# A two-layer decoder trunk in split float32: VectorE makes the low parts of all weight units, GpSimd none

## The reference

```python
for layer in range(DEPTH):                       # DEPTH = 2
    a = rmsnorm(h, attn_norm[layer])
    h = h + hybrid_mixer(a, w_in[layer], ..., w_out[layer])
    m = rmsnorm(h, ffn_norm[layer])
    if layer % 2 == 0:
        h = h + swiglu(m, dense_w_gate[i], dense_w_up[i], dense_w_down[i])
    else:
        h = h + moe_swiglu(m, router_w[i], moe_w_gate[i], moe_w_up[i], moe_w_down[i])
return rmsnorm(h, final_norm)

def swiglu(h, wg, wu, wd):
    return (jax.nn.silu(h @ wg) * (h @ wu)) @ wd
```

## Time and profile before

| | us |
|---|---|
| median of 3 runs | 2337.15 (2335.81 to 2337.19) |
| profiled execution, device time | 2332.12 |
| its span, first to last instruction | 2330.5 |
| mean granted clock of TensorE | 0.985 of full speed |

### The profile page before, as it was taken

One profiled execution on the slowest core, in us unless ns is written; L12 is line 12 of the kernel. 1 busy time (PEld: TensorE's weight loads), 2 busy tenths in 40 slices (PEclk: granted clock), 3 DMA queues, 4 the chain that ended last, 5 costly groups with the idle time before them and its releaser, 6 DMA issues.

```text
span 2330.5 us, 29151 instructions
## 1 busy us (share of the span) xinstructions
PE 2244.1 (96%) x10281; PEld 1830.2 (79%) x10281; DVE 1563.3 (67%) x1712; ACT 1239.3 (53%) x1529; POOL 383.4 (16%) x209
## 2 busy tenths in 40 slices
PE   7999999999999999999999999999979999999994
PEld 5888788888888888888877888877758777777773
DVE  4466675666655566666554457666769999989996
ACT  4445454454444344444444445444547777777774
POOL 2121212222222222222212121121200000000002
PEclk9999999999999999999999999999979999999997
DMA  6454535555555655555554445444669999999996
GB/s 225 159 169 156 181 127 182 170 174 198 183 195 180 201 192 185 196 195 183 181 180 162 163 146 179 154 172 163 215 236 378 375 373 387 379 378 374 373 383 220
DMA packets 261545, 525.46 MB, mean 225 GB/s; under 512 B 15044, under 2 KB 15144, under 8 KB 259944
## 3 DMA queue, kind: packets, MB, share of 16 engines
q1 hardware_dynamic: 248832, 497.33, 61.3%
q0 software_dynamic: 6256, 27.00, 3.1%
q10 hardware_dynamic: 6392, 0.25, 0.2%
HBM read 511.96 MB, written 15.73 MB: 226 GB/s over the span
## 4 chain that ended last, share of the span: by engine, by line
PE 77%; DVE 7%; DMA 7%; issue 4%; ACT 4%; POOL 1%; ACTq 0%; DVEq 0%; SPq 0%; POOLq 0%
PE acc L1399 20%; PE acc L1401 20%; PE acc L1400 20%; PE acc L1677 3%; PE acc L1679 3%; PE acc L1678 3%; DVE w_lo L893 3%; DMA raw<-in_moe_w_gate 2%; ACT w_hi L603 2%; DMA raw<-in_moe_w_up 2%; DMA raw<-in_moe_w_down 1%; PE X L1507 1%; PE X L1416 1%; PE X L1427 0%; PE X L1525 0%
## 5 line engine op out<-in xcount | busy, mean ns | idle before, releaser
L893 DVE TENSOR_TENSOR w_lo<-raw,w_hi 128x1024 fp32r<-128x1024 f32 x801 | 995.6, 1263 | 534.4 <-ACT w_hi L603 532.7
L603 ACT ACTIVATE w_hi<-raw 128x1024 fp32r<-128x1024 f32 x939 | 977.3, 1057 | 663.7 <-PE acc L1401 554.6
L1399 PE MATMUL acc<-w_hi,a_hi 128*128 128x512 f32 x1600 | 631.6, 395 | 8.6 <-POOL w_lo L510 4.7
L1401 PE MATMUL acc<-w_hi,a_lo 128*128 128x512 f32 x1600 | 625.3, 391 | 0.0
L1400 PE MATMUL acc<-w_lo,a_hi 128*128 128x512 f32 x1600 | 624.5, 390 | 0.0
L510 POOL TENSOR_TENSOR w_lo<-raw,w_hi 128x1024 fp32r<-128x1024 f32 x138 | 336.0, 2435 | 1333.8 <-ACT w_hi L603 1023.3
L1399 PEld LDWEIGHTS acc<-w_hi,a_hi 128*128 128x128 f32 x1600 | 301.7, 189 | 73.0 <-issue 6.8
L1401 PEld LDWEIGHTS acc<-w_hi,a_lo 128*128 128x128 f32 x1600 | 301.1, 188 | 63.9
L1400 PEld LDWEIGHTS acc<-w_lo,a_hi 128*128 128x128 f32 x1600 | 301.6, 188 | 60.3
L1677 PE MATMUL acc<-w_hi,a_hi 128*128 128x512 f32 x768 | 310.7, 405 | 8.9 <-DVE w_lo L893 7.9
L1679 PE MATMUL acc<-w_hi,a_lo 128*128 128x512 f32 x768 | 301.1, 392 | 0.0
(11 more groups left out here) (225 smaller groups left out, 1404.7 us busy)
## 6 DMA issues: line engine op xcount, KB each, us to landing
raw<-in_w_in SPq DMA_DIRECT2D x112, 1024.0 KB, 4.9
raw<-in_moe_w_gate SPq DMA_DIRECT2D x64, 1024.0 KB, 7.1
raw<-in_moe_w_up SPq DMA_DIRECT2D x64, 1024.0 KB, 5.7
raw<-in_moe_w_down SPq DMA_DIRECT2D x64, 1024.0 KB, 5.6
raw<-in_dense_w_gate SPq DMA_DIRECT2D x44, 1024.0 KB, 5.0
raw<-in_dense_w_up SPq DMA_DIRECT2D x44, 1024.0 KB, 5.0
raw<-in_dense_w_down SPq DMA_DIRECT2D x44, 1024.0 KB, 5.1
raw<-in_w_out SPq DMA_DIRECT2D x32, 1024.0 KB, 5.1
```

The source lines that it names most:

```text
L603: nc.scalar.activation(w_hi[:, slot], raw[:, tile % RAW_SLOTS, u % TILE_UNITS], ACT.Copy)\
L893: nc.vector.tensor_tensor(w_lo[:, slot], raw[:, (u // TILE_UNITS) % RAW_SLOTS, u % TILE_UNITS], w_hi[:, slot].bitcast(F32), ALU.subtract). ...
L1399: nc.tensor.matmul(dst, hi, w_hi[:, slot, c], start=first and c == 0, stop=False)
L1401: ins = nc.tensor.matmul(dst, lo, w_hi[:, slot, c], start=False, stop=last and c == UNIT_CHUNKS - 1)
```

## The change

GpSimd's loop of low parts goes, with its semaphore, and VectorE's `split_lo` no longer skips those units. One semaphore counts all low parts, so a waiter for unit `u` waits for `u + 1`.

```diff
-POOL_UNIT = 3
...
-        def pools(u):
-
-            return u < M0 and u % 4 == POOL_UNIT
-
         def low_ready(eng, u, per=0, i=None):
 
-            if u >= M0:
-                eng.wait_ge(lo_ready, lin(3 * M0 // 4 + u - M0 + 1, per, i))
-            elif pools(u):
-                eng.wait_ge(pool_ready, lin(u // 4 + 1, per // 4, i))
-            else:
-                eng.wait_ge(lo_ready, lin(3 * (u // 4) + u % 4 + 1, 3 * per // 4, i))
+            eng.wait_ge(lo_ready, lin(u + 1, per, i))
...
-            def low_parts(u, per, i):
-
-                pool.wait_ge(hi_ready, lin(u + 1, per, i))
-
-                low_ready(pool, u - 1, per, i)
-                nc.gpsimd.tensor_tensor(w_lo[:, u % SPLIT_SLOTS],
-                                        raw[:, (u // TILE_UNITS) % RAW_SLOTS, u % TILE_UNITS],
-                                        w_hi[:, u % SPLIT_SLOTS].bitcast(F32), ALU.subtract).then_inc(pool_ready, 1)
-
-            with pool.Fori(0, M0 // 8) as i:
-                low_parts(POOL_UNIT, 8, i)
-                low_parts(4 + POOL_UNIT, 8, i)
...
             def split_lo(u, per=0, i=None):
 
-                if pools(u):
-                    return
                 slot = u % SPLIT_SLOTS
```

More of the change, by code:

```diff
@@ L254, in trunk @@
         lo_ready = sem("lo_ready")
-        pool_ready = sem("pool_ready")
         used = sem("used")
```

## The result

The changed kernel takes 2351.6 us (median of 5 runs, 2344.3 to 2354.2) against 2335.8 for the kernel before beside it (5 runs); the ratio is 1.0063, with a 95% interval of 1.0045 to 1.0081. In a second set of runs it was 2350.4 against 2336.6, 1.0051 (1.0035 to 1.0067). So the change costs 12 to 15 us. The forecast was 2349, in a range of 2340.5 to 2357: direction, size and range held. Its terms held less well: the sum of them was 2 to 4 us short, and behind that stand misses of both signs; that is what the rest is about.

The account below looks back on a forecast made before the run. TensorE, busy 2244.1 of 2330.5 us, was taken to lose time only where it waits. The terms summed to +11.9 on the profiled 2332.1, giving 2344.0; with the 5.0 offset to the median, 2349, range 2340.5 to 2357.

Parts of the forecast that it names:

- Steady gate: Dense loop, ten trips: VectorE's longer queue makes its second add late, TensorE waits 0.56, 0.65 with restart: +6.5 us.
- First gate: Before the dense loop, once: one unit's length lost, +2.7 us, and a clock drop behind the 3.4 us gap, +1.7.
- Start: First weight tiles: GpSimd's spare-row copies, issued at 6 us, share the transfer engines; +5 us, bounds -1.4 to +9.
- rival 1: The start costs its upper end: +16 us in all, 2353; chance 0.17.
- Attention: Both layers, second and third quads: VectorE's chain and units gain 1.0 and 0.75 us per layer, together -3.5.
- Router: End of the second attention layer: VectorE's product no longer beside GpSimd's low part, router starts 0.5 us earlier: -0.5.
- Expert layer: Has no GpSimd low parts and was forecast to stay as it is.
- rival 2: The steady gate in the dense loop doesn't stall: +5.4 us in all, 2342.5; chance 0.15.
- rival 4: Only the gates pay: start near its lower end, no clock drop: +3.8 us in all, 2341; chance 0.12.
- rival 3: Not slower: VectorE freed of GpSimd's turns, start untouched, gate doesn't stall: -2.7 us, 2334.5; chance 0.08.

Follow-up runs that it names:

- Experiment 5: The changed kernel with GpSimd's copies held back and the dense loop gate's second reciprocal and product two units later: 2332.6 us, ratio 0.9973 to the kernel before.
- experiment 6: The control: the kernel before, GpSimd's low parts kept, with only the loop gate's second reciprocal and product two units later: 2337.0 us, ratio 1.0004.
- experiment 1: The changed kernel with GpSimd's three spare-row copies moved behind its wait for the end of both attentions: 2339.6 us, ratio 1.0008 to the kernel before.
- experiment 4: Against the kernel before, GpSimd keeps its low parts in both attention layers only (72 of 138), VectorE makes the dense layer's: 2348.4 us, ratio 1.0047.
- experiment 3: Against the kernel before, GpSimd keeps its low parts in the dense layer only (66 of 138), VectorE makes the attention's: 2326.2 us, ratio 0.9944.
- experiment 2: The kernel before with the three spare-row copies put ahead of GpSimd's loop of low parts, nothing else changed: 2346.8 us, ratio 1.0037.
- experiment 8: The changed kernel with copies held back, second reciprocal later and one low part inside the first gate: 2327.7 us, ratio 0.9950 to the kernel before.
- experiment 9: The kernel of experiment 8 run a second time: 2327.8 us, ratio 0.9959 to the kernel before.
- experiment 7: The changed kernel with copies held back and one low part between the first gate's two reciprocals: 2337.5 us, ratio 1.0003 to the kernel before.

## Why the prediction was right, and where it wasn't

*Steady gate: +6.5 forecast, +8.4 measured, mechanism shown.* The chain was right to 0.01 us, the wait 0.55 for 0.56. What was mis-sized is what a wait costs beyond itself: I took 0.09 for TensorE's restart, and it is 0.29 (each trip is 0.84 longer: 8.4 in ten). About half of that is how the trace counts: products here start 0.23 apart, so the one behind 582.12 was due at 582.35 and started 0.71 late, at 583.06, while the idle time in the row counts only from the end of the product before. The rest is that the next ones follow at 0.33 and 0.24 us. Experiment 5 removes it whole, the control shows that it is the order.

*First gate: +2.7 and +1.7 forecast, +5.6 measured.* The wait itself cost 2.7 (3.39 us between where the unit could have started and where it did, less the 0.67 of before). The granted clock fell as forecast, but the half clock lasted twice the 3.4 us forecast, in both executions of the kernel after; in experiments 1, 4 and 5, with the same wait, it lasted 3.4 (4.1 to 4.4 us lost in all). That this drop goes with the long wait is shown at this place: in five executions a wait of 3.2 us had it, in the eight others 1.45 us or less had none. A long wait isn't enough everywhere: in experiment 3 TensorE waited 3.46 us at the start (until 30.66), and the next 9 us were at full clock.

*Start: +5.0 forecast, +8.0 and +8.9 measured at unit 4.* This is the term that was mis-sized most: the upper end of its bounds, so rival 1 was right on the mechanism. I took 5 since "the first tile is nearly in by then". The first high part was indeed only 2.0 us late (13.90 for 11.88), but the second tile had all of the copies against it, and ScalarE's DMA issues stand behind its high part. The fourth high part came 8.50 us late (36.85 for 28.35), just the 8.5 us of extra traffic; but 7.0 of it came with the tile and only 1.5 with the issues, where the upper bound had all of it. Copies and weights did share by packets: 743 and 630 from 10 to 22 us, in packets of 3.9 and 2.0 KB (2.90 MB / 743, 1.25 MB / 630), so that the weights had 30% of the bytes. By the Trainium skill (DMA: Bandwidth & Descriptors, Queues, rings and completion order) engines go round the queues a packet at a time; the trace agrees with that (from 14 to 22 us the packets are 496 and 481), and the upper end that this would give is what came. Experiments 1 and 2 show the cause from both sides.

*Attention: -3.5 forecast; the sites forecast gave -4.8.* Per layer the unit at the second quad starts 1.62 us earlier after the one before it (3.08 us for 4.70) and that at the third 0.77 (3.08 for 3.85), in both layers alike. The second was forecast as 0.75. The first was forecast as 1.0, what the chain gains; but the transposes before the unit went from waiting 0.69 to not waiting, and behind them the unit's own wait and its restart went too. Experiment 3 keeps this gain, 4 gives it up.

*Router: -0.5 forecast, +0.5 of gain measured at the wait, 1.4 in all.* The product beside GpSimd's last low part took 3.19 us and 1.22 after. TensorE's wait ahead of the router's first transposes is 2.07 us in all four executions where GpSimd makes the low parts of the second attention (the kernel before, experiments 2, 4 and 6) and 1.57 in the nine others: the 0.5 of the forecast. What it left out is the clock. Right behind the longer wait the granted clock is at half its level for 3.4 us in each of those four (in the kernel before 0.50 from 1688.0 to 1691.4), and in none of the nine; without it and the 0.5, the transposes of the router's logits start 12.35 us behind unit 551 where it was 13.70, 1.4 earlier. Further on, each execution has one more long stretch at half the clock, of 17 to 24 us, whose length changes from one to the next; that is why experiment 4 gains 1.8 at units 552 to 554 without having the shorter wait.

*Expert layer: 0 forecast, +5.3 in the profiles.* Here the prediction had an unseen help. Of thirteen profiled executions the one of the kernel before had the shortest expert layer. All others are longer, by 1.8 to 8.1 us, among them experiments 2 and 6 (1.8 and 3.0), whose instructions are those of the kernel before but for one moved piece elsewhere. That profile was 5.0 below the median of its kernel, and I carried this 5.0 over as an offset. So the sum of the terms, +11.9, stands against +13.8 to +15.8 between medians and against +22.1 between the two profiled spans, and the difference is mostly the expert layer of one lucky execution. The five places as measured in the kernel after give 8.4 + 5.6 + 8.0 - 4.8 - 1.4 = +15.8: the losses were put too low by 6.1 and the gains by 2.2. That the forecast of 2349 came within 3 us is in part luck, since a third of the first miss was made good by the second, and 1.3 us more by the median of the kernel before, which was 2335.8 beside the change and 2337.15 in the forecast. The nine executions with VectorE alone in the attention had 2.3 to 8.1 there, the three others 1.8 to 3.0; whether some of it is the change's doing stays open.

*The clock.* Stretches at half the clock came in the attention of layer 0 as well, two of them (one is the window at 328 us above), at 1.4 and 1.6 us each, and the kernel before had none there; in layer 1 it was the other way round, one in the kernel before (1.6 us at unit 501) and none after. The control of experiment 6, with its attention unchanged, had two in layer 0 (1.3 and 1.6 at units 84 and 125) and lost the one at 501; so these belong to an execution and not to the change. Two executions of one kernel differ in it too: experiment 8 has one in layer 0, at 286 us, and experiment 9, the same kernel, has none.

Of the rivals, 1 had the start right, and with it a time of 2353, which is nearer to the first median (2351.6) than the forecast and less near to the second (2350.4). 2 to 4 fell: the gate stalls ten times out of ten, the start is touched, the clock drops, and the freedom from GpSimd's turns gave the attention's 4.8 us and the router's 1.4. Experiment 8 is what rival 3 would have needed: it is faster than before once its three places are mended. The Trainium skill's rule that VectorE and GpSimd take a shared port pair by turns (SBUF — State Buffer, Who interferes with whom) was quoted as speaking for a gain, for instructions of VectorE with two inputs. Rows with two inputs agree: the low part at 557.15 took 1.80 us beside GpSimd's for 1.21 without, the router's product 3.19 for 1.22. The slow small step of 2.32 us, which the prediction put under that rule, has one input (`sm`), so it isn't a case of the sentence quoted. The gain is real, and the sign for the whole was decided elsewhere.

## What to carry to other kernels

When work is taken off an engine, list what stood behind it in that engine's queue: here a loop of low parts had been the only thing that kept 3 MB of copies away from the first weights, and that was the largest single part of the loss. When work is put onto an engine with a third of its time free, the average says nothing; follow its queue at the two or three places where it also has a long operation and a deadline, and move the long operation behind the deadline. Before a profile's span is used as a base, look which of its stages is short against the median of the runs.

## What the runs showed of the hardware

- Two DMA queues with 3.9 KB and 2.0 KB packets had about as many packets each through (743 to 630 in 12 us, 496 to 481 in the last 8 of them), so the one with small packets had 30% of the bytes.
- ScalarE's three issues of thin weights took 5.9 us from the first one's start in the kernel before (17.90 to 23.80) and 8.7 in the kernel after (23.61 to 32.30), where the copies had ended by 23.76; in both the last issue ended 0.7 to 1.5 us behind the last packet of the weight queue (22.29 and 31.63). An issue is not a fixed price.
- A TensorE wait of 0.55 us in the trace made the trip 0.84 longer.
- VectorE's low part was 1220 ns on average without GpSimd's low parts and 1263 with them; a small operation of 0.16 us took 2.32 beside one.
- Behind 3.23 us of idle time TensorE ran the next 6.6 us at a granted clock of 0.55 (kernel after), and behind the same wait in experiment 1 only 3.4 us at half the clock; behind 1.45 us (experiment 7) it kept full speed, and so it did behind 3.46 us at the start of experiment 3.
- Ahead of the router a wait of 2.07 us was followed by 3.4 us at half the clock in four executions of four, one of 1.57 us by none in nine of nine.
